# Retention: the two tiles of squares of a head are added on VectorE before TensorE sums them

## The reference, cut to what matters

```python
def rms_norm_2(x, g):
    xf = x.astype(jnp.float32)
    y = xf * lax.rsqrt(jnp.mean(xf * xf, axis=-1, keepdims=True) + EPS)
    return (y * g.astype(jnp.float32)).astype(x.dtype)

def retention_mixer(q, k, v, g, decay_logit, gn_gain):
    ...
    fwd = retention_direction(q, k, v, log_gamma[0], False)
    bwd = ...
    y = rms_norm_2(fwd + bwd, gn_gain.reshape(RET_HEADS, RET_DV))
    y = y.reshape(Bn, S, RET_V).astype(dt)
    return jax.nn.silu(g) * y
```

## Time and profile before

| | |
|---|---|
| median of three runs | 1279.24 us |
| runs | 1278.44 to 1281.85 us |
| profiled execution | 1282.52 us |
| its span, first to last instruction | 1280.70 us |
| its mean granted TensorE clock | 0.995 of full |
| TensorE busy | 1257.1 us, 98% |
| VectorE busy | 924.3 us, 72% |
| ScalarE busy | 718.5 us, 56% |

### The profile page before, as it was taken

One profiled execution on the slowest core, in us unless ns is written; L12 is line 12 of the kernel. 1 busy time (PEld: TensorE's weight loads), 2 busy tenths in 40 slices (PEclk: granted clock), 3 DMA queues, 4 the chain that ended last, 5 costly groups with the idle time before them and its releaser, 6 DMA issues.

```text
span 1280.7 us, 20863 instructions
## 1 busy us (share of the span) xinstructions
PE 1257.1 (98%) x8064; PEld 1139.8 (89%) x8064; DVE 924.3 (72%) x1183; ACT 718.5 (56%) x1069; POOL 51.4 (4%) x77
## 2 busy tenths in 40 slices
PE   8999999999999999999999999999999999999999
PEld 7988899999999778999989899888888888888887
DVE  6889988886889658666675676566666677666665
ACT  3666744445744556444476764655555667655554
POOL 1101000000111000000001000000000000000000
PEclk8999999999999999999999999999999999999999
DMA  9986989996799724566647544456666552456650
GB/s 351 360 296 217 327 291 331 329 326 198 258 351 363 232 53 158 197 199 203 205 147 243 162 144 146 130 174 197 197 201 201 188 170 97 128 188 208 206 164 33
DMA packets 147135, 274.46 MB, mean 214 GB/s; under 512 B 4759, under 2 KB 85423, under 8 KB 146936
## 3 DMA queue, kind: packets, MB, share of 16 engines
q1 hardware_dynamic: 132176, 220.21, 51.4%
q0 software_dynamic: 13648, 51.01, 11.9%
q10 hardware_dynamic: 1240, 2.26, 0.5%
HBM read 272.36 MB, written 1.10 MB: 214 GB/s over the span
## 4 chain that ended last, share of the span: by engine, by line
PE 82%; DVE 8%; DMA 5%; ACT 3%; issue 2%; ACTq 0%; POOL 0%; DVEq 0%; POOLq 0%
PE ps L2164 81%; DMA ada_ring<-in_ada_w 4%; DVE wlo L1294 2%; DVE acc_a L1311 2%; ACT whi L541 1%; PE ps L2585 1%; PE ps L2318 1%; DMA voh<-in_voh 1%; ACT h L654 0%; DVE hboth L1476 0%; DVE x L1406 0%; ACT hboth L656 0%; ACT hboth L649 0%; PE ps L2693 0%; DVE xn L1420 0%
## 5 line engine op out<-in xcount | busy, mean ns | idle before, releaser
L1294 DVE TENSOR_TENSOR wlo<-raw,whi 128x1024 fp32r<-128x1024 f32 x400 | 484.5, 1225 | 231.3 <-ACT whi L541 230.6
L541 ACT CAST whi<-raw 128x1024 fp32r<-128x1024 f32 x400 | 416.7, 1049 | 416.4 <-PE ps L2164 401.1
L2164 PE MATMUL ps<-hboth,whi 128*128 128x256 f32 (+1 forms) x2720 | 607.2, 312 | 2.1 <-DVE wlo L1294 1.8
L2164 PE MATMUL ps<-hboth,wlo 128*128 128x256 f32 x1792 | 492.2, 275 | 4.1 <-DVE tmp L1598 3.8
L2164 PEld LDWEIGHTS ps<-hboth,whi 128*128 128x128 f32 x2720 | 447.7, 191 | 31.4 <-issue 5.0
L2164 PEld LDWEIGHTS ps<-hboth,wlo 128*128 128x128 f32 x1792 | 344.7, 192 | 6.6 <-DVE tmp L1598 4.4
L2164 PE MATMUL ps<-whi,hidhi 128*128 128x512 f32 x432 | 164.2, 380 | 0.0
L2164 PE MATMUL ps<-wlo,hidhi 128*128 128x512 f32 x432 | 163.7, 379 | 0.0
L2164 PE MATMUL ps<-whi,hidlo 128*128 128x512 f32 x432 | 163.7, 379 | 0.0
L2164 PE MATMUL ps<-whi,hboth 128*128 128x512 f32 (+1 forms) x512 | 155.5, 375 | 4.1 <-DVE wlo L1294 1.1
L2164 PEld LDWEIGHTS ps<-whi,hboth 128*128 128x128 f32 x512 | 95.2, 189 | 20.2 <-issue 7.3
(11 more groups left out here) (251 smaller groups left out, 1123.7 us busy)
## 6 DMA issues: line engine op xcount, KB each, us to landing
raw<-in_ffn_w_in SPq DMA_DIRECT2D x44, 1024.0 KB, 7.2
ada_ring<-in_ada_w POOLq DMA_DIRECT2D x40, 1024.0 KB, 8.1
raw<-in_w_mlp_up SPq DMA_DIRECT2D x32, 1024.0 KB, 5.3
raw<-in_w_mlp_down SPq DMA_DIRECT2D x32, 1024.0 KB, 4.9
raw<-in_ffn_w_out SPq DMA_DIRECT2D x22, 1024.0 KB, 5.1
raw<-in_att_w_qkv SPq DMA_DIRECT2D x18, 1024.0 KB, 6.7
raw<-in_w_in_even SPq DMA_DIRECT2D x18, 1024.0 KB, 5.1
raw<-in_hyb_w_in SPq DMA_DIRECT2D x10, 1024.0 KB, 12.6
```

Source lines behind the costliest of these rows:

```text
L541: A.copy(whi[:, H % 4, :], raw[:, slot(n), h * HALF:(h + 1) * HALF]).then_inc(s["hi_ready"], 1)
L1294: V.tensor_tensor(wlo[:, H % 4, :], raw[:, slot(n), h * HALF:(h + 1) * HALF], whi[:, H % 4, :].bitcast(F32), ALU.subtract).then_inc(s["lo_ ...
L2164: return pe.matmul(out, lhsT, rhs, start=first, stop=last, skip_group_check=True)
```

## The change

VectorE gets a new instruction for each head, `ret_add(h)`: it waits for the squares (`rt_sq`) and adds the second tile of squares onto the first, in place. TensorE's `ret_sums(h)` waits for that addition (`rt_added`) and multiplies ones with the one tile that is left. The other streams are unchanged.

```diff
+            def ret_add(h):
+
+                dve.wait_ge(s["rt_sq"], h + 1)
+                V.tensor_tensor(sq3[:, h % 2, 0:S], sq3[:, h % 2, 0:S], sq3[:, h % 2, S:512], ALU.add) \
+                    .then_inc(s["rt_added"], 1)
+
...
             ret_scores(1)
             next_split(8, 1)
             next_split(8, 2)
+            ret_add(0)
             ret_norm(0)
             ret_scores(2)
             next_split(8, 3)
 
+            ret_add(1)
             split(HX + 4)
             ret_norm(1)
             ret_scores(3)
             split(HX + 5)
+            ret_add(2)
             split(HX + 6)
             ret_norm(2)
             split(HX + 7)
+            ret_add(3)
             split(HX + 8)
             ret_norm(3)
             ret_gate(0)
...
             def ret_sums(h):
 
-                pe.wait_ge(s["rt_sq"], h + 1)
+                pe.wait_ge(s["rt_added"], h + 1)
                 if h:
                     pe.wait_ge(s["rt_r"], h)
-                for c in range(2):
-                    m = mm(ps[:, 3, 0:S], ones[:, :], sq3[:, h % 2, c * S:(c + 1) * S], c == 0, c == 1)
-                m.then_inc(s["rt_ssq"], 1)
+                mm(ps[:, 3, 0:S], ones[:, :], sq3[:, h % 2, 0:S]).then_inc(s["rt_ssq"], 1)
```

More of the change, by code:

```diff
@@ L81 @@
 even_in nr_sq nr_ssq nr_ln nr_r nr_done rp_rot rp_done
-dec_step dec_ready rt_sig rt_g rt_s rt_p rt_o rt_sq rt_ssq rt_ln rt_r rt_y rt_hi rt_lo
+dec_step dec_ready rt_sig rt_g rt_s rt_p rt_o rt_sq rt_added rt_ssq rt_ln rt_r rt_y rt_hi rt_lo
 sw_s sw_z sw_e sw_pn sw_t sw_tc sw_tl sw_o qkv_hi qkv_lo sw_sink sw_hi sw_lo
```

## The result

| | before | changed |
|---|---|---|
| median, 8 runs each | 1278.49 us | 1282.66 us |
| lowest to highest | 1277.69 to 1281.85 | 1280.96 to 1285.38 |
| profiled execution, time | 1282.52 | 1282.63 |
| its span | 1280.70 | 1280.80 |
| its mean granted clock | 0.995 | 0.992 |

The ratio is 1.0028 with a 95% interval from 1.0015 to 1.004, that is +3.6 us, between +1.9 and +5.1. It is an estimate over all runs and not the quotient of the two medians, which differ by 4.2 us; both lie in the interval. The kernel became slower by about as much as forecast: the difference is clear of noise, though just under the 0.3% from which the prediction calls it one.

What follows compares the result with a forecast made beforehand. The prediction took TensorE's instruction stream to bound the kernel there; +2.2 us from the heads and +1.5 from the clock gave +3.7, 1282.9 us beside the median of 1279.24, with an 8-in-10 range of 1279.8 to 1284.9.

Steps and rivals of the forecast that it cites:

- Head 0, the stall: At head 0's sums, TensorE waits some 2.8 us for an addition queued behind VectorE's split: +2.62 us, saving included.
- The addition: Each new VectorE addition of 128x256 f32 was taken to last 0.42 us.
- Head 1: At head 1's sums the addition ends about 0.3 us before TensorE asks, so the saving is kept: -0.43 us.
- Heads 2 and 3: Savings lost to TensorE's waits at ret_out(3) for ret_norm(2) and at even_out(8) for ret_lo(0): 0 each.
- Sum without the clock: The four heads' effects added, 2.62 - 0.43 - 0 - 0: +2.2 us.
- The clock: After TensorE's new stop at head 0 the granted clock falls to the 1.2 GHz level, costing 1.5 us.
- rival A: The stall at head 0 without a clock fall after it: +2.2 us, 1281.4; chance 0.22.
- the path of the forecast: Stall at head 0 with a clock fall behind it, later stops as profiled before: +3.7 us; chance 0.52.
- B: Clock falls at the new stop and also after the stop ending at 1115.80: +5.4 us, 1284.6; chance 0.13.
- C: No clock fall at the new stop, and the one from 856 on goes: +0.5 us, 1279.8; chance 0.10.
- D: Addition not behind the split, sums never wait, heads 0 and 1 save 0.43 each: -0.9 us, 1278.4; chance 0.03.

Runs made afterwards that it cites:

- e1: Changed kernel with VectorE's addition of head 0 moved ahead of the split of half (8,2); median 1279.10 us, ratio 0.9992 to the kernel before.
- e3: Kernel before plus one wait: TensorE's sums of head 0 wait for VectorE's split, no addition, no matmul saved; median 1282.93 us, ratio 1.0033.
- e5: Changed kernel with the addition only in heads 1 to 3, head 0 as before; distance 41.25 us, -0.42 against before; one run, 1279.12 us.
- e6: Changed kernel with the addition only in heads 2 and 3, the others as before; distance 41.69 us, +0.02 against before; one run, 1280.10 us.
- e4: Changed kernel with head 0's addition ahead of its split, and head 2's root and normalisation and ret_lo(0)'s two parts moved ahead of splits; 1276.70 us, ratio 0.9983.
- e9: Changed kernel, unchanged, profiled again to see how often the clock falls behind the new stop; 1287.48 us, distance 45.51 us.
- e11: Changed kernel, unchanged, profiled again for the clock behind the new stop; 1281.56 us, distance 43.85 us.
- e10: Changed kernel, unchanged, profiled again for the clock behind the new stop; 1281.09 us, distance 46.82 us.
- e2: Changed kernel with ten idle identity matmuls on TensorE ahead of the wait of head 0; median 1280.02 us, ratio 1.0006 to the kernel before.

## Why the prediction was right, point by point

**Head 0, the stall (+2.62 with its saving).** Right in kind and size: +2.62 is what the distance from ret_scores(1) to ret_scores(2) gives. The stop was forecast as some 2.8 us and is 2.78. The order that makes it was as read: split on ScalarE, split on VectorE, addition in the tail of the split (0.08 us before its end), TensorE 0.05 us later. From the end of the squares on, VectorE was idle or behind a wait for 3.2 us with the addition ready to run. e1 shows that its place in the queue is the cause, e3 that the wait alone gives the loss.

**The addition (0.42 us).** 0.421 us on average in the profile after.

**Head 1 (-0.43, kept).** Right: the changed kernel has -0.43 there, e5 as a whole -0.42, and neither the sums nor ret_out(2) wait. In the changed kernel the addition ends at 795.95, and TensorE loads the weights for the sums at 796.30; the slack is 0.35 us, or 0.3 with the 0.05 of the release, as forecast.

**Heads 2 and 3 (0 and 0, given back).** Right: the changed kernel has 0.00 for the two, e6 +0.02. e4 takes the two waits away and gets the savings. The idle time that the trace of before put down to no releaser was indeed the wait for ret_norm(2): e4 moved that instruction and the gap went.

**Sum without the clock (+2.2).** 2.18 in the distance; the rest in the table of means gives +2.2 as well, as an indication.

**The clock (+1.5, taken as the likelier).** Here the prediction chose badly at its place. Behind the new stop the clock fell in two of six profiles, not in most, and the mean of the six distances is 44.63, +2.96. The term should have been about 0.8 and not 1.5, and the likelier case at the new stop was rival A's, no fall, to which I gave 0.22. The failed step is "a stop of 2.8 us is longer than the one that was followed by a fall, so I take the fall as the likelier". One stop with and one without a fall, in one execution, can't carry that. That the measured +3.6 lies on the forecast of +3.7 doesn't prove the term, as its interval, +1.9 to +5.1, holds +2.2 and +3.0 as well, and it is in part luck. None of the six profiles took the path of the forecast, one fall behind the new stop and one behind the first MLP stop. Three came out at +3.8 to +3.9 by a path that I had in no rival: no fall behind the new stop, and one behind the second MLP stop where the profile of before had none. Their sum is 2.18 + 1.67, where the forecast has 2.2 + 1.5. The price of a fall was right: 1.60 in e3, 1.66 between e9 and the profiles without one.

**Rivals.** A is what happened at the new stop in four profiles of six, but in none of them for the whole program, since the falls behind the MLP stops were never those of the profile of before. B, a fall at the new stop and one behind the stop of the second MLP, happened in e9, whose falls behind the MLP stops begin at 860.0 and 1119.4. It was one case of six. C, no fall and none at the MLPs, is e11: +0.45 to the last matmul where +0.5 was forecast. e10 has none behind the MLPs either. D did not happen in the changed kernel; it is what e1 makes of it, -0.87 against the -0.9 forecast for it.

**Open.** Behind the two MLP stops the six profiles of the changed kernel have eight falls in twelve chances, the seven of all other kernels four in fourteen. It may be that the new delay changes how the later stops lie to whatever the clock goes by, and this would be where a part of the 1.2 us goes; no run tests it. It may also be chance, as the two falls of one execution aren't independent. It was not settled. Nor is it settled why e2 loses less to the clock than the kernel before, which has no stop there at all.

## What to carry to other kernels

When work is moved from a busy engine to an idle one, ask what it will stand behind in the idle engine's queue, not how much time that engine has: here 0.42 us of work on an engine that idled for 3 us made the busy engine stop for 2.8 us, and moving the instruction one place up turned the loss of 2.18 us over the four heads into a gain of 0.87. A matmul saved is worth only what the next wait behind it leaves, so look for the first instruction downstream that starts just behind its releaser and move that releaser too. Compare a distance inside the program between two traces when the change is small, since here whole executions differed by more than the change before they reached it.

## What the runs showed of the hardware that was not expected

The same stop of 2.78 us was followed by no fall of the granted clock (four profiles), by a fall of 3.4 us (e9) and by one of 6.8 us that began within the stop (e10), so a stop has no fixed price: +2.18, +3.84 and +5.15 us in the same place. The rule of the Trainium skill that the prediction weighed (page "TensorE: Matmul & The Clock Gate", section "Why this matters for your kernels", no gaps over about 3 us) is not safe on this side: gaps of 2.78 and 2.45 us were followed by a fall, though the same gap of 2.78 us had none in the other four profiles.

A stop on TensorE also costs a little at its end, which the prediction had read from the earlier trace rows and the changed kernel bears out. Behind its stop the load of weights and the first matmul both start at 788.12 and the second matmul 0.32 us later, while before, with no stop, the load for the sums started at 788.75, 0.11 us ahead of the first matmul at 788.86, and the matmuls followed each other by 0.22 us. That the load couldn't be done in advance may be the reason; it fits these times, and no run tests it.
